# A new common order of projections and S5 in the mixer of a one-core layer kernel, masks on ScalarE, a later memory norm, a shorter GELU

## What is computed

```python
def s5_mixer(...)          # u -> diagonal complex state space, then GELU and a gated linear unit
def rwkv7_mixer(...)       # r, k, v, z projections, token shift, decays, 64x64 states
def memory_kv(mem, g_mem, w_mem_kv):
    m = rmsnorm(mem, g_mem) @ w_mem_kv
    mk, mv = jnp.split(m, 2, axis=-1)
...
def layer(x, mem_k, mem_v, h0_re, h0_im, prev, s0, P, l):
    n1 = rmsnorm(x, P['norm_mix_g'][l])
    proj = n1 @ P['w_in'][l]
    u = proj[..., :S5_WIDTH]
    prk = proj[..., S5_WIDTH:]
    s5_y, h_re, h_im = s5_mixer(u, ...)
    rw_y, shift_last, s_final = rwkv7_mixer(prk, prev, s0, ...)
    x = x + jnp.concatenate([s5_y, rw_y], axis=-1) @ P['w_out'][l]
    x = x + cross_attention(rmsnorm(x, P['norm_ca_g'][l]), mem_k, mem_v, P['w_cq'][l], P['w_co'][l])
    h = rmsnorm(x, P['norm_ffn_g'][l]).reshape(bsz * t, D_MODEL)
    x = x + moe_ffn(h, ...).reshape(bsz, t, D_MODEL)
```

## Time and profile before

| | us |
|---|---|
| median of three runs | 1476.4 |
| the profiled execution, its own time | 1477.95 |
| span of its trace | 1476.2 |
| TensorE busy in the span | 1380.8 (94%) |
| VectorE busy | 451.5 (31%) |
| ScalarE busy | 240.8 (16%) |
| GpSimd busy | 63.8 (4%) |
| mean granted TensorE clock | 0.975 |

### The profile page before, as it was taken

One profiled execution on the slowest core, in us unless ns is written; L12 is line 12 of the kernel. 1 busy time (PEld: TensorE's weight loads), 2 busy tenths in 40 slices (PEclk: granted clock), 3 DMA queues, 4 the chain that ended last, 5 costly groups with the idle time before them and its releaser, 6 DMA issues.

```text
span 1476.2 us, 21161 instructions
## 1 busy us (share of the span) xinstructions
PE 1380.8 (94%) x8649; PEld 699.1 (47%) x8649; DVE 451.5 (31%) x892; ACT 240.8 (16%) x460; POOL 63.8 (4%) x118
## 2 busy tenths in 40 slices
PE   6987899999998999999999899898999998998997
PEld 4666568866665543343343343343333433433342
DVE  6987664534312231211211221121112111211112
ACT  3111242112213122011011011010010110110102
POOL 3633100000000000000000000000000000000000
PEclk9998889999999999999999999999999999999999
DMA  8971011004658769999999999999999999999993
GB/s 321 176 167 58 29 64 59 31 31 147 270 215 335 298 240 399 399 421 429 427 428 429 428 428 427 429 429 428 428 428 428 427 429 428 429 426 426 428 424 140
DMA packets 43335, 471.84 MB, mean 320 GB/s; under 512 B 4992, under 2 KB 10368, under 8 KB 11520
## 3 DMA queue, kind: packets, MB, share of 16 engines
q1 hardware_dynamic: 37264, 461.42, 75.3%
q10 hardware_dynamic: 6000, 9.41, 3.4%
HBM read 465.33 MB, written 5.48 MB: 319 GB/s over the span
## 4 chain that ended last, share of the span: by engine, by line
PE 66%; DMA 20%; DVE 11%; issue 2%; ACT 1%; SPq 0%; ACTq 0%; DVEq 0%
DMA big<-in_w_gu 19%; PE bank L1179 15%; PE bank L1228 14%; PE bank L711 7%; PE bank L1102 5%; PE bank L969 2%; PE bank L794 2%; PE bank L1292 2%; PE bank L1248 2%; PE bank L888 1%; DVE big L1818 1%; PE bank L1109 1%; PE bank L1204 1%; PE bank L1277 1%; DVE big L1853 1%
## 5 line engine op out<-in xcount | busy, mean ns | idle before, releaser
L1179 PE MATMUL bank<-big 128*64 128x512 f32 x1920 | 428.9, 603 | 30.3 <-DMA big<-in_w_gu 29.8
L1179 PEld LDWEIGHTS bank<-big 128*64 128x64 f32 x1920 | 143.6, 138 | 312.5 <-issue 300.6
L1228 PE MATMUL bank<-big 128*64 128x512 f32 x960 | 209.4, 594 | 0.0
L711 PE MATMUL bank<-big 128*128 128x320 f32 (+1 forms) x688 | 187.1, 430 | 2.3 <-ACT big L1493 1.3
L711 PEld LDWEIGHTS bank<-big 128*128 128x128 f32 x688 | 130.8, 192 | 56.4 <-issue 5.2
L2208 DVE TENSOR_TENSOR big<-big,bank 128x320 f32<-128x320 f32 x120 | 58.5, 487 | 304.0 <-PE bank L1248 298.7
L2194 DVE TENSOR_SCALAR big<-bank 128x512 f32<-128x512 f32 x32 | 22.2, 693 | 395.5 <-PE bank L1179 365.4
L1228 PEld LDWEIGHTS bank<-big 128*64 128x64 f32 x960 | 69.9, 137 | 128.2 <-issue 126.3
L1562 ACT ACTIVATE big<-big 128x512 f32<-128x512 f32 x30 | 18.8, 626 | 452.4 <-DVE big L2194 452.4
L1343 ACT ACTIVATE big<-bank 128x320 f32<-128x320 f32 (+3 forms) x122 | 53.2, 436 | 238.9 <-PE bank L880 40.1
L1102 PE MATMUL bank<-big 128*128 128x512 f32 x192 | 87.1, 603 | 1.4 <-DVE big L2142 1.4
(11 more groups left out here) (411 smaller groups left out, 1164.4 us busy)
## 6 DMA issues: line engine op xcount, KB each, us to landing
big<-in_w_gu SPq DMA_DIRECT2D x128, 2048.0 KB, 25.1
big<-in_w_down SPq DMA_DIRECT2D x62, 2048.0 KB, 22.2
big<-in_dense SPq DMA_DIRECT2D x47, 1024.0 KB, 8.5
big<-u_windows ACTq DMA_DIRECT2D x32, 160.0 KB, 9.1
big<-in_w_down SPq DMA_DIRECT2D x4, 1024.0 KB, 17.4
big<-in_smw SPq DMA_DIRECT2D x1, 1408.0 KB, 19.4
big<-in_xT SPq DMA_DIRECT2D x2, 640.0 KB, 4.6
big<-in_consts SPq DMA_DIRECT2D x1, 1028.5 KB, 14.6
```

The costliest lines, as they stand in the source:

```text
L711: last = mm(b[:, 0:n], w[:, k, :], src[:, k, :], start=(k == 0), stop=(k == kt - 1))
L1179: last = mm(ps[n][part, :], xte[:, 2 * j + k, part], w[s][:, k, n * 512:n * 512 + 512], start=False, stop=end)
L1228: last = mm(ps[bank][part, :], actT[:, 4 * d + i, part], w[s][:, i, h * 512:h * 512 + 512], start=(d == 0 and i == 0), stop=end)
```

## The change

1. `MIX_ORDER` is a new list. All entries of S5 are spread between single projection tiles; the last v tiles and the LoRA come before memk, and the six memk tiles stand together ahead of glu.
2. `mask_windows` leaves VectorE (one operation of 128 x 2560) and goes to ScalarE (seven operations of 128 x 320 on every eighth element, each scaled by one column of the mask). TensorE waits for seven signals for each window.
3. The memory's squares go from GpSimd to ScalarE. Its sums, its roots and `mem_norm` become entries of the list (memsum, memtotal, memroot, memnorm), and `mem_norm` stands near the end.
4. GELU takes three VectorE operations after the sum where it took five; the last (`s5_gated`) is an entry of its own, and the factor of one half moves into glu, on ScalarE as a scale and on VectorE as a second multiplier.
5. `mixes` of z is split into a delta and three shares; `k_norm` is taken into `decays`, with its root's wait behind other work; the fourth tile of u is read out earlier; a memset goes to GpSimd.

```diff
-MIX_ORDER = ([("load", 0), ("load", 1), ("f", 0), ("memnorm", 0), ("c", 0)] + _tiles("in", "k", 0, 2) + [("par", 0)] + _tiles("in", "k", 2, 4)
-             + [("win", 0), ("blk", 0), ("mix", "k"), ("scan", 0), ("load", 2), ("y", 0), ("f", 1)] + _tiles("in", "z", 0, 4)
-             + [("win", 1), ("mix", "z"), ("par", 1), ("blk", 1), ("load", 3), ("scan", 1), ("out", 0)] + _tiles("in", "r", 0, 1)
-             + [("gelu", 0), ("c", 1)] + _tiles("in", "r", 1, 2) + [("win", 2), ("y", 1)] + _tiles("in", "r", 2, 4)
-             + [("par", 2), ("out", 1), ("blk", 2), ("scan", 2), ("mix", "r")] + _tiles("in", "v", 0, 1) + [("gelu", 1)] + _tiles("in", "v", 1, 2)
-             + [("c", 2), ("win", 3), ("y", 2)] + _tiles("in", "v", 2, 4) + [("par", 3), ("out", 2), ("blk", 3), ("c", 3), ("scan", 3), ("y", 3)]
-             + [("mix", "v"), ("lora_up", 0), ("gelu", 2), ("memk", 0), ("memk", 1), ("out", 3), ("kk", 0), ("knorm", 0), ("gelu", 3), ("memk", 2),
-                ("lora_down", 0), ("memk", 3), ("decays", 0), ("memk", 4), ("decay_exp", 0), ("memk", 5), ("glu", 0)])
+MIX_ORDER = [("in", "k0"), ("memsum", 0), ("load", 0), ("in", "k1"), ("f", 0), ("in", "k2"), ("load", 1), ("c", 0), ("in", "k3"),
+             ("par", 0), ("memtotal", 0), ("win", 0), ("in", "z0"), ("f", 1), ("blk", 0), ("scan", 0), ("y", 0), ("in", "z1"), ("load", 2),
+             ("memroot", 0), ("mix", "k"), ("in", "z2"), ("win", 1), ("out", 0), ("par", 1), ("in", "z3"), ("c", 1), ("blk", 1), ("gelu", 0),
+             ("scan", 1), ("gated", 0), ("y", 1), ("in", "r0"), ("load", 3), ("delta", "z"), ("in", "r1"), ("shares", 0), ("shares", 1),
+             ("out", 1), ("par", 2), ("c", 2), ("in", "r2"), ("win", 2), ("blk", 2), ("shares", 2), ("scan", 2), ("y", 2), ("gelu", 1),
+             ("gated", 1), ("in", "r3"), ("in", "v0"), ("mix", "r"), ("out", 2), ("par", 3), ("in", "v1"), ("win", 3), ("c", 3), ("gelu", 2),
+             ("gated", 2), ("blk", 3), ("scan", 3), ("y", 3), ("lora_up", 0), ("in", "v2"), ("in", "v3"), ("kk", 0), ("memnorm", 0),
+             ("out", 3), ("gelu", 3), ("mix", "v"), ("gated", 3), ("lora_down", 0), ("knorm", 0), ("decays", 0), ("memk", 0),
+             ("decay_exp", 0), ("memk", 1), ("memk", 2), ("memk", 3), ("memk", 4), ("memk", 5), ("glu", 0)]
...
-                pe.wait_ge(S("uwin"), ct + 1)
+                pe.wait_ge(S("uwin"), (BL - 1) * (ct + 1))
...
                 if kind == "in":
                     dense_stream(FIRST["in"] + 2 + 2 * IN_ORDER.index(n[0]), int(n[1]), n, n1, T)
+                elif kind == "memsum":
+                    pe.wait_ge(S("consts_in"), 16)
+                    partial_sums("pa_m", memsq, NM, ones, "memsq")
+                elif kind == "memtotal":
+                    total_sums("ss_m", "pa_m", rm, ones)
...
+            def norm_parts(dst, nm):
+
+                copy(dst, f"pa_{nm}", lambda b: b[:, 0:dst.shape[-1]])
+
+            def norm_roots(dst, nm, signal):
+                inverse_root(dst, computed(act, f"ss_{nm}")[:, 0:dst.shape[-1]], 1.0 / (32 * D), eps_rms, signal, f"ss_{nm}")
+
             def norm_factors(dst, nm, signal):
-
-                n = dst.shape[-1]
...
+            act.wait_ge(S("mem_in"), 16)
+            for k in range(KT):
+                step(af(memsq[:, k, :], memT[:, k, :], ACT.Square), "memsq")
             stored(act, "u3")
             act.wait_ge(S("u_pad"), 1)
             act.dma_start(u_dram.ap().rearrange("(c p) t -> p c t", p=P), uT).then_inc(S("u_stored"), 16)
...
-            norm_factors(view(KKO, NM), "m", "rm")
+            def mask_windows(ct):
+
+                act.wait_ge(S(f"uwin_in{ct % 2}"), 16 * BL * (ct // 2 + 1))
+                w = uwins[ct % 2].rearrange("p g t -> p (g t)")
+                for j in range(BL - 1):
+                    step(af(w[:, j::BL], w[:, j::BL], ACT.Identity, scale=con("window")[:, j:j + 1]), "uwin")
+
             act.wait_ge(S("u_stored"), 16)
+            act.wait_ge(S("consts_in"), 16)
...
-                    inverse_root(R[9], R[9], 1.0, None, "kk_norm")
+                    inverse_root(R[15], R[15], 1.0, None, "kk_norm")
...
+                        step.read_out(af(view(UWIN, CT, T)[:, i, :], b[:, 0:T], ACT.Sigmoid, scale=0.5, bias=vec("s5_glu_b", i)), f"gl{i}")
...
-            pool.wait_ge(S("mem_in"), 16)
-            for k in range(KT):
-                step(tt(memsq[:, k, :], memT[:, k, :], memT[:, k, :], ALU.mult), "memsq")
+            step(nc.gpsimd.memset(view(KKO, 256), 0.0), "kk_zero")
...
             u_rows(2)
+            u_rows(3)
...
-            u_rows(3)
...
-            def mixes(c):
+            def delta(c):
 
...
-                outs = [(R[4], 3), (R[5], 4), (R[6], 5)] if c == "z" else [(p, "rkv".index(c))]
-                for dst, mu in outs:
-                    for i in TILES4:
-                        last = stt(dst[:, i, :], DELTA[:, i, :], vec("rwkv_mu", 4 * mu + i), p[:, i, :], mul, add)
-                        step(last, "z_mixed" if c == "z" else ("delta_free" if (c, i) == ("v", 3) else None))
+
+            def share(c, dst, mu):
+                for i in TILES4:
+                    last = stt(dst[:, i, :], DELTA[:, i, :], vec("rwkv_mu", 4 * mu + i), prj[c][:, i, :], mul, add)
+                    step(last, "z_mixed" if c == "z" else ("delta_free" if (c, i) == ("v", 3) else None))
+
+            def mixes(c):
+                delta(c)
+                share(c, prj[c], "rkv".index(c))
...
-            def mask_windows(ct):
-
-                dve.wait_ge(S(f"uwin_in{ct % 2}"), 16 * BL * (ct // 2 + 1))
-                step(tt(uwins[ct % 2], uwins[ct % 2], over(con("window"), 1, 8), mul), "uwin")
-
...
-                step(tt(z, yl[ct], yl[ct], mul))
-                step(ts(z, z, 0.044715, 1.0, mul, add))
-                step(tt(z, z, yl[ct], mul), "gelu_arg")
+                step(stt(z, yl[ct], 0.044715, yl[ct], mul, mul))
+                step(stt(z, z, 1.0, yl[ct], add, mul), "gelu_arg")
+
+            def s5_gated(ct):
+
                 dve.wait_ge(S("gelu_tanh"), ct + 1)
-                step(stt(z, z, 1.0, yl[ct], add, mul))
-                step(ts(z, z, 0.5, None, mul), "s5_gelu")
+                step(stt(mix[:, ct, :], mix[:, ct, :], 1.0, yl[ct], add, mul), "s5_gelu")
...
-            def k_norm():
-                for i in TILES4:
-                    b = computed(dve, f"kn{i}")
-                    step.read_out(ts(R[9][:, i, :], b[:, 0:T], 1e-24, None, ALU.max), f"kn{i}")
-                dve.wait_ge(S("kk_norm"), 1)
-                step(tt(kk, kk, R[9], mul))
-
...
                 stored(dve, "dw3")
                 for i in TILES4:
                     step(v.tensor_tensor_scan(R[13][:, i, :], con("carry"), R[3][:, i, :], 0.0, mul, add), "decay_sums" if i == 3 else None)
+                for i in TILES4:
+                    b = computed(dve, f"kn{i}")
+                    step.read_out(ts(R[15][:, i, :], b[:, 0:T], 1e-24, None, ALU.max), f"kn{i}")
                 stored(dve, "da3")
-                computed(dve, "kn3")
                 for i in TILES4:
                     ka, one = vec("rwkv_k_a", i), view(SCAN + 700, 1)
                     step(ts(one, ka, -1.0, 1.0, mul, add))
                     step(ts(R[6][:, i, :], a_[:, i, :], ka, one, mul, add))
                 step(tt(k, k, R[6], mul))
+                dve.wait_ge(S("kk_norm"), 1)
+                step(tt(kk, kk, R[15], mul))
                 step(tt(R[6], kk, a_, mul))
...
-                    step(tt(mix[:, i, :], mix[:, i, :], view(UWIN, CT, T)[:, i, :], mul), "s5_gated")
+                    step(stt(mix[:, i, :], mix[:, i, :], 0.5, view(UWIN, CT, T)[:, i, :], mul, mul), "s5_gated")
...
+                elif kind == "delta":
+                    delta(n)
+                elif kind == "shares":
+                    share("z", R[4 + n], 3 + n)
...
+                elif kind == "gated":
+                    s5_gated(n)
```

More of the change, by code:

```diff
@@ L225, in job_names @@
 def job_names():
-    yield from ["pa_x", "u0", "ss_x", "u1", "u2", "u3", "pa_m", "ss_m"]
+    yield from ["pa_x", "u0", "ss_x", "u1", "u2", "u3"]
     for kind, n in MIX_ORDER:
@@ L232, in job_names @@
             yield n
+        elif kind == "memsum":
+            yield "pa_m"
+        elif kind == "memtotal":
+            yield "ss_m"
         elif kind == "blk":
@@ L413, in build @@
         Rc = [view(at, CT, NC, CH) for at in RW]
-        xsq, memsq = view(UWIN, KT, T), view(RW[8], KT, NM)
+        xsq, memsq, rm = view(UWIN, KT, T), view(RW[8], KT, NM), view(MK, NM)
         xg, first_ones = view(RW[4], KT, T), view(MIX, P)
@@ L728, in _ @@
                 dense_stream(FIRST["in"], i, f"u{i}", xg, T)
-            pe.wait_ge(S("consts_in"), 16)
-            partial_sums("pa_m", memsq, NM, ones, "memsq")
-            total_sums("ss_m", "pa_m", view(KKO, NM), ones)
             pe.wait_ge(S("n1"), KT)
@@ L1351, in inverse_root @@
                 step(af(dst, dst, ACT.Exp, scale=-0.5), signal)
```

(28 more changed lines are left out.)

## The result

The changed kernel takes 1463.7 us (median of four runs, 1463.18 to 1464.14) against 1475.45 us for the kernel before; the ratio is 0.9924, with an interval of 0.9912 to 0.9935. It is faster by 11.7 us where 25.0 was forecast. The profiled execution took 1463.18 us, with a span of 1461.4.

A forecast was written before the change was run, and what follows sets the result against it. TensorE bounds the mixer, with holes from VectorE's queue. Without holes bo ends at 175.1 us; plus 1.4 + 4.9 + 4.9 + 0.6, 4.8 clock, 1.5 gaps: 193.2, 25.0 before 218.2, so 1451.4 us (range 1446 to 1456, chance 0.50).

The forecast's parts named there:

- The two holes: TensorE waits 4.9 us twice for ScalarE's masks, directly ahead of blocks 2 and 3, at 95 and 120 us.
- gaps: On TensorE in the mixer, gaps between jobs of different kinds add 1.5 us.
- Glu's weights: Chunk 14 comes some 2 us before glu starts: no cost while that cover holds, up to 3 us without.
- Window 0: Its loads land at 45 to 48 us; it is masked at about 53.6, just as z0 ends, so no hole.
- Part 1: The mixer's start: k0 at 27.45 us, u's store at about 30, window loads from about 35, z0's end at 53.6.
- rival A: Window 0 or masks late: landing at 54 us, TensorE loses 5 us, gain 10 to 15, 1463 to 1466; chance 0.17.
- The mask: On ScalarE, seven operations at 0.60 us make a mask of 4.3 us, with ends of 3.3 and 5.3.
- The clock: TensorE at half clock behind the two holes of 4.9 us: 2.4 us each, 4.8 in all, ends 0 and 10.
- VectorE off the path: In the mixer, VectorE's queue no longer holds TensorE up, except at the end, where kn waits some 0.6 us.
- Part 3: VectorE's work in the mixer: some 17 us less with masks gone and GELU shorter, so it leaves TensorE's path.
- Rival C: VectorE stays on TensorE's path; the 8.1 and 4.6 us waits come back, gain 12, 1464 us; chance 0.09.
- The stages behind: From bo's end to the span's end, the stretch stays as long as now, 1258.0 us, to 1 us.

The follow-up runs named there:

- the one on the kernel before: The kernel before with only the masks moved to ScalarE, in the old order of the list: 1476.7 us, ratio 1.0009.
- the fastest kernel: The changed kernel with SyncE's loads held back from u's store and window 0, masks of windows 2 and 3 earlier, gelu 1 ahead of c 2: 1443.2 us, ratio 0.9782.

## Why the prediction was wrong

**What held.** The mixer is a TensorE stage with holes, and VectorE's queue made them: its waits are gone. k0 began behind u3 without a gap. The two holes that the change makes, directly ahead of blocks 2 and 3, are there; they begin at 109.2 and 138.4 us, where 95 and 120 were named, mostly because block 0 was already 9.4 us late. TensorE was busy for 154.1 us in the mixer, where 147.6 of work, 4.8 for the clock and 1.5 for gaps make 153.9. Glu's weights cost nothing: no wait of TensorE's shows there. The later stages have no clock of their own: by the medians, each kernel that ended bo earlier was faster.

**Window 0.** This is the largest term: block 0 at 63.0 us and not at 53.6, 9.4 of the 14.8 us by which bo was late (208.0 against 193.2). Of the 9.4, 8.9 are the wait, and z0 ended 0.5 us late. Two steps of Part 1 failed. The store was priced by the row in which nothing else ran: it was issued at 28.97 us, 4.6 us earlier than before, which put it beside chunk 4 (issued at 28.23), and the loads went at 37.33 where about 35 was forecast. And the loads were given a landing at 45 to 48 us, from a row without SyncE's transfers, though m0 and chunk 5 were seen to move beside them. That was rival A, which had 0.17 and named 54 us for the landing and 1463 to 1466 for the time. It was the right mechanism with too small a chance, and it came with a part that it did not have, the store. That its time was met is in part luck: it had 5 us for the wait where 8.9 were lost.

**The mask.** It took 6.3 to 6.4 us and not 4.3. The two holes were 6.9 and 6.9 us where 4.9 was forecast: 4.0 us. Rival A had 5.3 us as its upper end; the operation went past it. VectorE's ratio of 1.37 was not the right guide for ScalarE, whose ratio is 1.65 for the stride alone (0.780 to 0.472), and the scale from a column was given nothing.

**The clock.** 4.8 us were taken for two holes. There were three. Behind block 0's the clock was 0.50, behind block 2's and 3's 0.59 and 0.50; the blocks took 4.2, 3.8 and 4.2 us against the 2.5 at full clock, and the tile at 81.58 took 6.25 us at 0.61, without a wait of its own ahead of it. Together that is about 1.7 + 1.3 + 1.7 + 1.9 = 6.6 us, and the work right behind blocks 0 and 3 lost another 0.6 and 0.4: an estimate of 7.6, some 3 more than forecast. The 2.4 us for a hole of 4.9 was itself not wrong: in the run with contiguous masks, a hole of 4.8 cost 2.6. But the price doesn't go by the length of the hole, as 1.3 behind one of 6.9 shows. Windows of 3 us, columns as in the earlier trace rows:

```profile
62.00:65.00 3.00, 2.03 (x36) 1.95 (x40) 0.00 (x0) 1.32 (x3) 0.00 (x0) 0.50 1.12 139
...
83.00:86.00 3.00, 3.00 (x8) 1.99 (x7) 2.93 (x3) 2.90 (x4) 2.84 (x3) 0.61 1.01 123
117.00:120.00 3.00, 3.00 (x39) 1.64 (x36) 2.07 (x5) 0.44 (x1) 1.02 (x3) 0.59 0.03 5
146.00:149.00 3.00, 3.00 (x40) 1.66 (x36) 1.36 (x4) 0.44 (x1) 0.98 (x2) 0.50 0.02 5
```

**VectorE off the path.** Part 3 was right for the kernel as it is (one wait of 0.8 us), and wrong for the reason it gave. It followed the signals and not the banks: v0 needs st1's bank. With the masks' holes closed that is 7.1 us. Rival C, with 0.09, was there all the time behind rival A.

**The account.** TensorE's waits were 180.6 - 154.1 = 26.5 us, where 1.4 + 4.9 + 4.9 + 0.6 = 11.8 was forecast: 14.7 us more, of which block 0 is 8.9, the two masks 4.0, the bank 0.8, and block 1 1.0 (0.9 for its parameters and 1.5 for its mask, where 1.4 was forecast). Its busy time was 0.2 more. That is the whole of the 14.8 us. Inside the busy time three errors cancel, which is luck: the clock took about 3 us more, the 1.5 us for gaps did not show, and the work must then have been about 1 us less than 147.6.

**The stages behind.** From bo's end to the end of the span it is 1253.4 us, and 1258.0 before; the forecast said the same to 1 us. That was a sign of the forecast, and it failed by 4.6 us. Nothing shows this to be an effect of the change: the same stretch, with the same instructions, is between 1252.3 and 1256.3 us in the experiments, 1254.9 in the one on the kernel before, whose other executions have spans of 1470.4 to 1475.9 us where the profiled one has 1476.2. So the profiled span fell by 14.8 us, 10.2 of them in the mixer. The medians fell by 11.7.

## What to carry to other kernels

A step that is moved off a busy engine must also be placed: directly ahead of its reader on the new engine it is a new hole, and the same move lost 6 us in one kernel and gained 6 in another, with the list and the loads around it changed. When a wait is taken away, look at what is second, and follow the banks as well as the signals. And price a transfer by a row in which the same other queue is busy: the store and the loads took up to twice as long beside weights that nobody needed yet.

## What the runs showed of the hardware

A ScalarE operation of 128 x 320 from SBUF to SBUF took 0.472 us contiguous, 0.780 with every eighth float, 0.562 with the scale from a column, and 0.872 with both. The store of 654 KB took 3.6 us alone and 7.5 us beside one 1 MB load of another queue. Behind waits of TensorE of 4.8 to 8.9 us the granted clock was 0.50 to 0.59, and a block of small matmuls took 3.8 to 4.2 us and not 2.5. The stages behind bo, which no edit touched, varied from 1252.3 to 1258.0 us between executions, and the four runs of the fastest kernel from 1440.0 to 1448.5. A gain of 5 us in a 215 us stage is seen better in the trace, which tells it to some 2 us, than in the median.
